# Input norm in two halves of 264 tokens, first weight unit behind two input tiles, one DMA addition and one fill product placed earlier

## The reference

```python
def rmsnorm(x, g):
    y = x * lax.rsqrt(jnp.mean(x * x, axis=-1, keepdims=True) + EPS)
    return y * g

def swiglu(h, w_gate, w_up, w_down):
    return (jax.nn.silu(h @ w_gate) * (h @ w_up)) @ w_down

h = jnp.concatenate([meta, x], axis=1)          # (1, 528, 1024)
h = h + 0.5 * swiglu(rmsnorm(h, ffn1_norm), ffn1_w_gate, ffn1_w_up, ffn1_w_down)
h = h + token_mixing(rmsnorm(h, mix_norm), ...)
h = h + 0.5 * swiglu(rmsnorm(h, ffn2_norm), ffn2_w_gate, ffn2_w_up, ffn2_w_down)
return rmsnorm(h, final_norm)[:, N_META:]
```

## Time and profile before

| | |
|---|---|
| median of the runs | 1034.66 us (1034.66 to 1034.73) |
| the profiled execution | 1034.95 us |
| its span, first to last instruction | 1033.2 us |
| TensorE (PE) busy | 1024.9 us, 99% of the span |
| VectorE (DVE) busy | 739.9 us, 72% |
| ScalarE (ACT) busy | 541.3 us, 52% |
| GpSimd (POOL) busy | 465.2 us, 45% |
| chain that ended last, TensorE's share | 93% |
| granted TensorE clock | 0.999 of full speed |

### The profile page before, as it was taken

One profiled execution on the slowest core, in us unless ns is written; L12 is line 12 of the kernel. 1 busy time (PEld: TensorE's weight loads), 2 busy tenths in 40 slices (PEclk: granted clock), 3 DMA queues, 4 the chain that ended last, 5 costly groups with the idle time before them and its releaser, 6 DMA issues.

```text
span 1033.2 us, 20279 instructions
## 1 busy us (share of the span) xinstructions
PE 1024.9 (99%) x7693; PEld 950.5 (92%) x7693; DVE 739.9 (72%) x1288; ACT 541.3 (52%) x892; POOL 465.2 (45%) x571
## 2 busy tenths in 40 slices
PE   9999999999999999999999999999999999999997
PEld 8999999999999999889868788878899999999997
DVE  7977667787665588599975584578877766666735
ACT  7555545445454354563456527544555554554536
POOL 5444345354343367259931304455444433433440
PEclk9999999999999999999999999999999999999999
DMA  7777776787876544335321102222767887777732
GB/s 225 147 181 179 168 176 150 167 158 161 192 145 147 140 105 125 90 87 143 98 73 34 49 15 82 68 74 84 173 145 165 178 182 178 163 169 179 156 90 82
DMA packets 195108, 137.54 MB, mean 133 GB/s; under 512 B 8643, under 2 KB 179702, under 8 KB 195014
## 3 DMA queue, kind: packets, MB, share of 16 engines
q1 hardware_dynamic: 178208, 97.38, 33.9%
q0 software_dynamic: 16704, 38.80, 22.4%
q10 hardware_dynamic: 102, 0.08, 0.0%
HBM read 91.18 MB, written 2.10 MB: 90 GB/s over the span
## 4 chain that ended last, share of the span: by engine, by line
PE 93%; DVE 3%; DMA 2%; ACT 1%; issue 1%; POOL 1%; SPq 0%; DVEq 0%; POOLq 0%; ACTq 0%
PE ps L2670 43%; PE ps L2905 36%; PE ps L633 4%; PE ps L780 1%; PE ps L954 1%; PE ps L831 1%; PE ps L810 1%; PE ps L715 1%; DMA wxl<-raw 1%; POOL wl L1913 1%; DMA xin<-in_x 1%; DVE xn L2605 1%; DVE xl L2610 0%; PE ps L843 0%; PE ps L995 0%
## 5 line engine op out<-in xcount | busy, mean ns | idle before, releaser
L1913 POOL TENSOR_TENSOR wl<-raw,wh 128x256 fp32r<-128x256 f32 x196 | 154.3, 836 | 186.5 <-ACT wh L2070 132.0
L1941 POOL DMA_DIRECT2D wxl<-raw x78 | 66.9, 859 | 254.3 <-ACT wxl L2075 253.2
L2670 PE MATMUL ps<-ah,wxh 128*128 128x264 f32 (+2 forms) x464 | 123.3, 319 | 0.8 <-DMA wxl<-raw 0.7
L2670 PE MATMUL ps<-ah,wxl 128*128 128x264 f32 (+2 forms) x464 | 123.0, 318 | 0.0
L2670 PE MATMUL ps<-al,wxh 128*128 128x264 f32 (+2 forms) x464 | 122.9, 318 | 0.0
L2670 PE MATMUL ps<-xh,wh 128*128 128x264 f32 (+3 forms) x400 | 114.4, 335 | 0.0
L2670 PE MATMUL ps<-xl,wh 128*128 128x264 f32 (+3 forms) x400 | 110.5, 325 | 0.0
L2670 PE MATMUL ps<-xh,wl 128*128 128x264 f32 (+3 forms) x400 | 110.2, 324 | 0.0
L2905 PE MATMUL ps<-xh,wh 128*128 128x264 f32 (+1 forms) x380 | 107.6, 283 | 0.0
L2905 PE MATMUL ps<-xl,wh 128*128 128x264 f32 (+1 forms) x380 | 107.6, 283 | 0.0
L2905 PE MATMUL ps<-xh,wl 128*128 128x264 f32 (+1 forms) x380 | 107.1, 282 | 0.0
(11 more groups left out here) (334 smaller groups left out, 3057.2 us busy)
## 6 DMA issues: line engine op xcount, KB each, us to landing
raw<-in_ffn_w_gate SPq DMA_DIRECT2D x44, 512.0 KB, 5.3
raw<-in_ffn_w_up SPq DMA_DIRECT2D x44, 512.0 KB, 5.2
raw<-in_ffn_w_down SPq DMA_DIRECT2D x80, 256.0 KB, 4.0
wxl<-raw POOLq DMA_DIRECT2D x60, 256.0 KB, 4.1
raw<-in_w_in SPq DMA_DIRECT2D x28, 512.0 KB, 4.2
wxl<-raw POOLq DMA_DIRECT2D x21, 512.0 KB, 5.2
wl<-raw POOLq DMA_DIRECT2D x19, 512.0 KB, 5.2
raw<-in_w_out SPq DMA_DIRECT2D x8, 512.0 KB, 3.4
```

The source lines that it names most:

```text
L1913: op = pool.tensor_tensor(dst[:, part], src[:, part], high[:, part].bitcast(F32), ALU.subtract)
L1941: pool.dma_start(places(1, PLACE[u], c)[:, 0:n], raw[:, u % RING, 0:n], accum_op=ALU.add).then_inc(low_added[e], 16)
L2670: mm = pe.matmul(ps[0:m, bank + a, 0:width], places(lo, PLACE[u], -(-WIDTH[u] // HALF_UNIT))[:, k * P:k * P + m], r[:, tile, t:t + width], ...
```

## The change

- The input norm runs in two halves of 264 tokens: `norm_x(half)` and `low_x(half)` on VectorE (eight steps each, in the order norm 0, copy, invert, copy, low 0, norm 1, h_done, low 1) and `high_x(half, d)` on ScalarE. The spread sums are made per half. x_hi, x_lo and xn_done now count to 16.
- Diagonals: GpSimd makes that of tile 0 only; ScalarE makes those of tiles 1 and 2 after the first root, and 3 and 4 later. The first inverse comes after three copies instead of four. ScalarE keeps both halves of tile 4.
- SyncE issues the load of weight unit 0 ahead of tiles 3 and 4 of x.
- GpSimd rounds units 0 and 1, each in halves that are announced by themselves; ScalarE no longer rounds unit 1. ScalarE's order after it is: round unit 2, xh of half 1, negate 2, round 3, negate 3.
- TensorE: 8 warm-up products instead of 10, no `keep_warm`. `first_products` takes half 0 of units 0 and 1 as its inputs arrive, with the turns of tile 4 and the second spread between, then half 0 of unit 2, waits for h_done, and then does half 1 and the rest.
- `add_low(first)` of the first pair of FFN 1 stands between the second and the third subtraction.
- In the attention one fill step of p = 0 stands ahead of logits(1).

```diff
@@ lay_out
         for v, place in enumerate(([14, 12, 10, 8], [2, 4, 6, 0, 2, 4, 8, 10])[number]):
             put(u + v, place, 2, split=0 if number == 0 and v >= 2 else 2)
-        if number == 0:
-            for v in (2, 3):
+            if number == 0 and v >= 2:
                 add_by_dma(u + v, v - 2, 2)
@@ banks
-        X_BANKS, VEC_BANK = 6, 4
-        X_BY_ACT = 8
+        X_BANK, VEC_BANK = [0, 1, 2, 3, 4, 5, 4, 5, 1, 3], 7
+        X_BY_ACT = (8, 9)
@@ pe_mixer
             for p in range(PAIRS):
+                if p == 0:
+                    fill_step(KT)
                 if p + 1 < PAIRS:
                     pe.wait_ge(lg_done, 2 * p + 2)
                     logits(p + 1)
...
-                if not fill_first:
+                if p and not fill_first:
                     fill_step(KT + 2 * p)
                 fill_step(KT + 2 * p + 1)
@@ sync
             load_x(0)
             load_x(1)
-            load_x(2)
-            load_x(3)
...
                         load(u0 + 2 * f + e, v[:, :, f * P:(f + 1) * P], cols())
+                        if (number, f, e) == (0, 0, 0):
+                            load_x(2)
+                            load_x(3)
@@ gpsimd
-                        if (g, m) in SOON:
+                        if (g, m) in SOON or (number, g, m) == (0, 1, 0):
                             lo_pair(U_PAIR[number, g, m], lambda: add_low(first))
...
-            for t in range(X_PARTS[0].stop):
-                pool.tensor_tensor(diag[:, t, :], ident[:, :], xvar[:, t:t + 1].broadcast_to([P, P]), ALU.mult).then_inc(x_diag_pool, 1)
+            pool.tensor_tensor(diag[:, 0, :], ident[:, :], xvar[:, 0:1].broadcast_to([P, P]), ALU.mult).then_inc(x_diag_pool, 1)
...
+            for u in range(2):
+                pool.wait_ge(w_in_slot[u], 16)
+                for c in range(2):
+                    hi_half(u, c)
+                for c in range(2):
+                    lo_half(u, c)
@@ scalar
+            x_square(1)
+            x_square(2)
+            x_roots(0)
+            act.wait_ge(x_inv, 2)
+            act.wait_ge(x_turned, 6)
+            for t in range(1, 3):
+                act.activation(diag[:, t, :], ident[:, :], ACT.Copy, scale=xvar[:, t:t + 1]).then_inc(x_diag, 1)
+            x_square(3)
+            for d in range(4):
+                high_x(0, d)
+            x_square(4)
             x_roots(1)
-
+            high_x(0, 4)
+            high_x(0, 5)
             act.wait_ge(x_inv, 3)
             for t in range(3, 5):
                 act.activation(diag[:, t, :], ident[:, :], ACT.Copy, scale=xvar[:, t:t + 1]).then_inc(x_diag, 1)
+            high_x(0, 6)
+            high_x(0, 7)
+            for n in X_BY_ACT:
+                keep_x(act, n)
+            act.wait_ge(w_hi, Q_HI[1])
+            hi(2)
             for d in range(KT):
-                high_x(d)
-                if d == 1:
-                    act.wait_ge(w_hi, Q_HI[0])
-                    act.wait_ge(w_in_slot[1], 16)
-                    second_unit_half(0)
-                elif d == 4:
-                    second_unit_half(1)
-            hi(2)
+                high_x(1, d)
+            negative(2)
             hi(3)
-            negative(2)
             negative(3)
@@ vector
+            def norm_x(half):
+                part = slice(half * HALF, (half + 1) * HALF)
+                dve.wait_ge(x_kept, 6 + 2 * half)
+                if half:
+                    dve.wait_ge(x_kept_act, 2)
+                dve.wait_ge(x_spread, half + 1)
+                for d in range(KT):
+                    dve.scalar_tensor_tensor(out=xn[:, d // 4, 4 + d % 4, part], in0=h[:, d, part],
+                                             scalar=gains[:, 0, d:d + 1], in1=ps[:, 6 + half, 0:HALF], op0=ALU.mult,
+                                             op1=ALU.mult).then_inc(xn_done, 1)
+
+            def low_x(half):
+                part = slice(half * HALF, (half + 1) * HALF)
+                for d in range(KT):
+                    dve.wait_ge(x_hi, KT * half + d + 1)
+                    dve.tensor_tensor(xl[:, d, part], xn[:, d // 4, 4 + d % 4, part], xh[:, d, part].bitcast(F32),
+                                      ALU.subtract).then_inc(x_lo, 1)
+
+            norm_x(0)
+            keep_x(dve, 6)
+            invert_x(1)
+            keep_x(dve, 7)
+            low_x(0)
+            norm_x(1)
+            dve.wait_ge(x_kept, 8)
+            dve.wait_ge(x_kept_act, 2)
             dve.sem_inc(h_done, KT)
+            low_x(1)
@@ tensor, first_products
+                pe.wait_ge(x_kept, 3)
+                for k in range(4):
+                    part(0, k, 0, False, 0)
+                for k in range(4):
+                    part(0, k, 1, False, 0)
+                turn_x(8)
+                turn_x(9)
+                for k in range(4, 6):
+                    part(0, k, 0, False, 0)
+                    part(0, k, 1, False, 0)
+                for k in range(4):
+                    part(1, k, 0, False, 0)
+                spread(1)
+                for k in range(6, KT):
+                    part(0, k, 0, False, 0)
+                    part(0, k, 1, False, 0)
+                for k in range(4, KT):
+                    part(1, k, 0, False, 0)
+                parts(0, 0, True, 0)
+                parts(1, 1, False, 0)
+                parts(1, 0, True, 0)
+                pe.wait_ge(x_kept, 7)
+                parts(2, 0, False, 0)
+                pe.wait_ge(h_done, KT)
+                for k in range(KT):
+                    for v in range(2):
+                        for lo in range(2):
+                            part(v, k, lo, False, 1)
+                parts(2, 0, False, 1)
+                parts(0, 0, True, 1).then_inc(w_used, 2)
+                parts(1, 0, True, 1).then_inc(w_used, 2)
...
```

More of the change, by code:

```diff
@@ L2264, in _, with x_square @@
             act.wait_ge(consts, 1)
-            for t in range(1, 5):
+            def x_square(t):
                 act.wait_ge(x_loaded[t], 16)
@@ L2608, in _ @@
-            for d in range(KT):
-                dve.wait_ge(x_hi, d + 1)
-                dve.tensor_tensor(xl[:, d, :], xn[:, d // 4, 4 + d % 4, :], xh[:, d, :].bitcast(F32),
-                                  ALU.subtract).then_inc(x_lo, 1)
+            dve.wait_ge(vecs_kept, 1)
+            def norm_x(half):
[8 more added lines that the diff above has]
+                                             op1=ALU.mult).then_inc(xn_done, 1)
@@ L2692, in first_products, with part @@
             def first_products(u):
-                def part(v, k, lo, low_x=False):
+                def part(v, k, lo, low_x, half):
                     if low_x:
-                        pe.wait_ge(x_lo, k + 1)
-                    elif k == 0 and lo and u + v in BY_DMA:
+                        pe.wait_ge(x_lo, KT * half + k + 1)
+                    elif v < 2:
+                        if k % 4 == 0:
+                            pe.wait_ge(w_split if lo else w_hi, (Q_END if lo else Q_HI)[u + v] - 1 + k // 4)
+                    elif lo:
@@ L2708, in part @@
-                    if v == 3 and k == 0 and not lo and not low_x:
-                        pe.wait_ge(xn_done, KT)
-                    for a, t, width in parts_of(0):
-                        mm = pe.matmul(ps[:, 2 * v + a, 0:width], places(lo, PLACE[u + v], 2)[:, k * P:(k + 1) * P],
-                                       (xl if low_x else xh)[:, k, t:t + width], start=(k == 0 and not lo and not low_x),
-                                       stop=(k == KT - 1 and low_x))
-                    return mm
@@ L2732, in first_products @@
-                for v, lo in ((1, 1), (2, 0), (3, 0)):
-                    for k in range(KT):
-                        part(v, k, lo)
-                low_inputs(0)
-                low_inputs(1)
-                for v in (2, 3):
-                    for k in range(KT):
-                        part(v, k, 1)
-                    low_inputs(v)
+                        pe.wait_ge(w_hi, Q_HI[u + v])
+                    if not lo and not low_x:
+                        pe.wait_ge(x_hi, KT * half + k + 1)
@@ new lines, in part, with parts @@
+                    return pe.matmul(ps[:, 2 * v + half, 0:HALF], places(lo, PLACE[u + v], 2)[:, k * P:(k + 1) * P],
+                                     (xl if low_x else xh)[:, k, half * HALF:(half + 1) * HALF],
+                                     start=(k == 0 and not lo and not low_x), stop=(k == KT - 1 and low_x))
+                def parts(v, lo, low_x, half):
+                    for k in range(KT):
+                        mm = part(v, k, lo, low_x, half)
+                    return mm
@@ new lines, in first_products @@
+                parts(0, 0, True, 1).then_inc(w_used, 2)
+                parts(1, 0, True, 1).then_inc(w_used, 2)
+                pe.wait_ge(xn_done, 2 * KT)
+                parts(3, 0, False, 0)
+                parts(3, 0, False, 1)
+                for v in (2, 3):
```

(23 more changed lines are left out.)

118 lines of the change are left out of this document (47 added, 71 removed).

## The result

| | before | after |
|---|---|---|
| median | 1034.76 us (8 runs, 1034.66 to 1035.07) | 1036.84 us (8 runs, 1036.02 to 1039.29) |
| ratio, 95% interval | | 1.0024 [1.0015, 1.0034] |
| the profiled execution | 1034.95 us, span 1033.2 | 1036.02 us, span 1034.2 |

The changed kernel is 0.24% slower, against 0.2% that a measurement can tell. Its profiled execution is the shortest of its eight and only 1.07 us above that of before. The first question is thus where the 1.07 comes from, the second why the eight runs spread over 3.3 us where those of before spread over 0.4.

A forecast was written before the change was run, and what follows sets the result against it. TensorE, busy 99% of the span, was taken as the bound. Start +2.4, old stall −0.83, new wait +0.7 and fill product +0.06 made +2.3 on 1034.66: 1037.0 us, range 1033.5 to 1038.9.

The forecast's parts named there:

- the collision: At the start, VectorE's first four half 0 low parts each wait behind one GpSimd unit 1 subtraction: 4 × 0.69 us.
- The start: First four weight units: first product at 11.4 us, but VectorE's chain ends last, next group at 40.1 against 37.68: +2.4 us.
- h_done: Signal after half 1's normalisation, for which TensorE waits ahead of half 1: at 23.6 us, or 20.9 without a collision.
- The old stall: At 42 us TensorE waits for the DMA addition into the low weights; issued sooner, its 0.83 us goes.
- The new wait: TensorE's second group waits for GpSimd's last two subtractions, queued behind the DMA, with a VectorE turn between: +0.7 us.
- The fill product: Attention, fill product ahead of logits(1): the 0.24 us wait moves on to logits(2), +0.06 us; bounds −0.24 and +0.47.
- the clock: Rival, chance 0.15: TensorE's clock falls as it runs eight matmuls from 16.9 to 20.2 us; costs 1.8, giving 1038.8 us.
- No turns: Rival, chance 0.25: GpSimd's unit 1 subtractions miss or don't hold up the narrow low parts; 1034.3 us.
- Start kept: Rival, chance 0.10: VectorE keeps ahead at the start, TensorE's group ends at 36.4, −1.3 us; total 1032.3 us.

The follow-up runs named there:

- both variants without the collision: Changed kernel with zeros written as unit 1's low part, 1034.39 us; changed kernel with GpSimd's unit 1 subtractions held until VectorE's half 0 low parts end, 1034.47 us.
- half 1 let in: Changed kernel with GpSimd's unit 1 subtractions held back, h_done ahead of the second norm and unit 1's low weights behind 32 matmuls of half 1: 1034.39 us.
- fillers: Extra 128-column matmuls into a free bank around half 0's low products: changed kernel, plus two warm-ups, 1036.76 us; changed kernel with GpSimd's unit 1 subtractions in 128-column pieces, 1036.91 us.

## Why the prediction came out as it did

The total, 1037.0 against 1036.84 us, is nearer than its terms, and that is in part luck: the sum was made for the profiled execution, where +2.3 was forecast and +1.07 came, and what brings the median near are runs that the sum didn't have. The direction and the main cause, the collision, were right. Point by point:

- **The start, +2.4.** VectorE's chain was right up to its low parts: first product near 11.4 (11.51), low parts from 14.7 (14.88), halves at 0.41 and 0.34 a step. The term mis-sized is the collision, 4 × 0.69 = 2.76; it measured 1.83 turn about and 2.43 with GpSimd first. I had taken a turn to be the whole of both instructions (1.03); it is 0.89, and three full ones and two of 0.45 came, not four.
- **h_done.** "It waits for low parts and then for h_done" didn't come: behind the last low product TensorE had 24 matmuls to do, 2.9 us, and reached half 1 at 22.75 by itself, just as VectorE's second norm ended (19.47 + 3.27 = 22.74). The price was the same for another reason, as that work also stands behind the low parts. Group at 39.36, not 40.1: **+1.68**. The remedy follows: the collision had to be taken away, not h_done moved.
- **The old stall, −0.83:** right; −0.77 in the changed kernel, −0.78 alone. The way there was off: ScalarE's negated weights waited for their load, so the addition was issued at 38.23 (36.55 on the clock of before, told 35.3). It was in time because it took 5.52 us, not 5.93.
- **The new wait, +0.7:** wrong; 0. The step that failed is the turn left to VectorE between GpSimd's last two subtractions. In every profiled execution that has the line GpSimd did them on end. The text had this as a case ("if VectorE takes no turn in between it is 0") and took the other. The mechanism was in the rows only for turn about; GpSimd first shows in no row of before.
- **The fill product, +0.06:** 0.05 and 0.04 in the traces; the wait of 0.24 moved one step, as told. One end was added up wrong, without weight in the sum: 519.40 + 1.25 is 520.65, not 520.75.
- These terms give 1.68 − 0.77 + 0.04 = +0.95 for the profiled execution, against 1.07; by the product at 83.64, 1.07 behind its like of before, 0.16 more had been lost since 43.79. The other **+1.0** of the median is put down to what the forecast didn't have, the second pattern (0.65), and to what it kept apart as a rival with 0.15, the clock (1.8 told, 1.5 measured). This is argued from the runs' times and from traces of other runs; of the first eight only the shortest has a trace. The rival was right in place and in what it costs; it comes in some runs, not in all or none, so as a case of its own it was badly put. It lies in the tail (six of 19 runs above 1037.9, one of them with a clock of 0.999); two sets of runs of the changed kernel have medians of 1036.84 and 1036.40, with the tail's share the likely reason.
- **No turns** (1034.3): this is what both variants without the collision give, 1034.39 and 1034.47. Right price, wrong condition: 264-wide subtractions do take turns.
- **Start kept** (1032.3): nothing near it was seen. One reason is that the first four products run at ScalarE's 0.40 us a step, which I had left out: even with the collision gone and half 1 let in, the group came at 37.52, not 36.4.

## What to carry to other kernels

A step moved to an idle engine is priced by what it meets there: list the two-input SBUF instructions of VectorE and GpSimd by time, and shift one of them beside an instruction that reads PSUM. Where a change makes TensorE run one matmul per step of another engine, look at the spread of the runs, not at one profile: five of the changed kernel's 19 had a lowered mean clock, and none of 21 with a few fillers had, though on other chips as far as they are named. Test each edit alone; here one line was the gain (−0.74 us), and the new start paid it away.

## What the runs showed of the hardware

- The collision of VectorE (two SBUF inputs, 264 columns) and GpSimd has two patterns. Turn about: a step is GpSimd's instruction plus 0.2 us (0.89 with 256 columns, 0.61 with 128). GpSimd first: it runs all that it has queued without a gap, three of 0.69 or seven of 0.42, and the record of one VectorE instruction, 0.42 us by itself, lasts 2.85 or 3.42 with its wait. VectorE came 0.49 to 0.50 us after GpSimd's first start where they took turns and 0.49 to 0.51 after it where GpSimd went first, so its distance doesn't tell them apart; what decides is open and was not tried. The Trainium skill (SBUF — State Buffer, "Who interferes with whom") has the first to issue hold the pair for its whole instruction, and issue order decide who blocks. Turn about agrees with that. GpSimd first doesn't, if the records' starts tell the issue: without the sooner addition VectorE's record starts at 14.94, ahead of GpSimd's second at 15.12, and yet it waited for three.
- The 1.2 GHz rate came back in the middle of a kernel, behind a wait of 0.56 us and eight matmuls 0.34 us apart, and in another execution with the same wait and matmuls it didn't; of the 21 runs with fillers and the 31 without the collision none had a clock below 0.998.
